# Starting the result's rows as routing weights times the down projection's biases in a fused mixer and expert layer

## The reference

```python
logits = xt @ w_router + b_router                 # 1024 tokens, 32 experts
top_val, top_idx = lax.top_k(logits, 4)
top_w = softmax(top_val)
# each (token, expert) pair, in blocks of one expert:
gate = min(xblk @ w_gate[e] + b_gate[e], 7)
up = clip(xblk @ w_up[e] + b_up[e], -7, 7)
h = (up + 1) * gate * sigmoid(1.702 * gate)
yb = h @ w_down[e] + b_down[e]
y = segment_sum(yb * row_w, row_tok)              # sum over a token's four experts
x = x + gt2 * rms_norm(y, g_post_ffn)
```

## Time and profile before

| | us |
|---|---|
| median of three runs | 2683.56 (2679.57 to 2684.94) |
| the profiled execution | 2680.95 |
| its span, first to last instruction | 2679.1 |
| PE busy | 2422.3 (90%) |
| DVE, ACT, POOL busy | 921.2, 486.7, 413.7 |
| mean granted clock of TensorE | 0.963 of full |

### The profile page before, as it was taken

One profiled execution on the slowest core, in us unless ns is written; L12 is line 12 of the kernel. 1 busy time (PEld: TensorE's weight loads), 2 busy tenths in 40 slices (PEclk: granted clock), 3 DMA queues, 4 the chain that ended last, 5 costly groups with the idle time before them and its releaser, 6 DMA issues.

```text
span 2679.1 us, 35693 instructions
## 1 busy us (share of the span) xinstructions
PE 2422.3 (90%) x11737; PEld 1214.5 (45%) x11784; DVE 921.2 (34%) x1880; ACT 486.7 (18%) x1097; POOL 413.7 (15%) x376
## 2 busy tenths in 40 slices
PE   5999999977884899999999999999999999999992
PEld 3575766663452444444443334433444444434430
DVE  3144536571465222313322233222333323222224
ACT  4121222222441110101110111111111111010111
POOL 5000000004000112111112122122221212212122
PEclk9999999999986899999999999999999999999996
DMA  9112120205022768595899979979877898989875
GB/s 329 32 40 79 40 79 16 87 29 209 32 114 82 253 226 272 157 307 180 269 362 315 321 241 342 356 262 352 260 257 266 292 355 275 332 310 303 310 256 176
DMA packets 213755, 587.60 MB, mean 219 GB/s; under 512 B 20010, under 2 KB 79778, under 8 KB 213698
## 3 DMA queue, kind: packets, MB, share of 16 engines
q1 hardware_dynamic: 131698, 338.21, 34.7%
q10 hardware_dynamic: 53200, 193.02, 20.3%
q0 software_dynamic: 28800, 55.59, 9.8%
HBM read 548.47 MB, written 38.27 MB: 219 GB/s over the span
## 4 chain that ended last, share of the span: by engine, by line
PE 84%; DVE 9%; issue 3%; ACT 1%; POOL 1%; DMA 1%; DVEq 0%; ACTq 0%; SPq 0%; POOLq 0%
PE ps L1582 24%; PE ps L1608 14%; PE ps L1640 12%; PE ps L1658 7%; PE ps L1362 4%; PE ps L1466 4%; PE ps L1358 3%; PE ps L1365 2%; PE ps L1422 2%; PE ps L1551 2%; PE ps L1368 1%; PE ps L1618 1%; PE ps L1334 1%; PE ps L1540 1%; PE ps L1600 1%
## 5 line engine op out<-in xcount | busy, mean ns | idle before, releaser
L1582 PE MATMUL ps<-w_gate_e,xT 128*128 128x512 f32 x736 | 345.8, 592 | 0.0
L1582 PE MATMUL ps<-w_up_e,xT 128*128 128x512 f32 x736 | 345.8, 592 | 0.0
L1640 PE MATMUL ps<-w_down_e,hT 128*128 128x512 f32 x736 | 319.6, 592 | 0.0
L1216 DVE TENSOR_SCALAR oh_gu<-part_e,tab_e 128x128 bf16<-128x128 f32 x48 | 13.9, 290 | 852.1 <-PE ps L1582 543.3
L571 POOL DMA_INDIRECT xg<-xn_rows,gidx x49 | 51.0, 1041 | 1553.5 <-DVE sidx_tab L1207 1490.5
L797 ACT ACTIVATE sig_sb<-gate_sb 128x1024 f32<-128x1024 f32 x47 | 49.7, 1057 | 1160.0 <-DVE gate_sb L1222 1140.5
L1608 PE MATMUL ps<-w_gate_e,xT 128*32 128x256 f32 (+1 forms) x1504 | 236.1, 486 | 0.0
L1608 PE MATMUL ps<-w_up_e,xT 128*32 128x256 f32 (+1 forms) x1504 | 229.9, 474 | 0.0
L1582 PEld LDWEIGHTS ps<-w_up_e,xT 128*128 128x128 f32 x736 | 139.8, 190 | 176.0 <-issue 176.0
L1640 PEld LDWEIGHTS ps<-w_down_e,hT 128*128 128x128 f32 x736 | 139.8, 190 | 168.3 <-issue 165.0
L1582 PEld LDWEIGHTS ps<-w_gate_e,xT 128*128 128x128 f32 x736 | 139.8, 190 | 168.3 <-issue 165.0
(11 more groups left out here) (308 smaller groups left out, 2591.5 us busy)
## 6 DMA issues: line engine op xcount, KB each, us to landing
w_down_e<-in_w_down_dram ACTq DMA_DIRECT2D x368, 512.0 KB, 4.6
w_gate_e<-in_w_gate_dram SPq DMA_DIRECT2D x256, 512.0 KB, 5.6
w_up_e<-in_w_up_dram SPq DMA_DIRECT2D x256, 512.0 KB, 6.8
w_ring<-in_w_ada_dram SPq DMA_DIRECT2D x17, 1024.0 KB, 5.4
w_ring<-in_w_in_dram SPq DMA_DIRECT2D x20, 512.0 KB, 5.1
w_first<-in_w_ada_dram SPq DMA_DIRECT2D x7, 1024.0 KB, 12.5
y_rows<-box POOLq DMA_DIRECT2D x10, 512.0 KB
x_all<-in_x_dram SPq DMA_DIRECT2D x2, 2048.0 KB, 10.7
```

The lines of the kernel that those rows point to most:

```text
L1582: last = T.matmul(ps[:, b, :], xT[:, k, :], wgt[b // 2][:, k, (b % 2) * 512:(b % 2) * 512 + 512], start=False, stop=k == KT - 1)
L1640: last = T.matmul(ps[:, 4 + b, :], hT[:, k, :], wgt[2][:, k, b * 512:b * 512 + 512], start=False, stop=k == KT - 1)
```

## The change

`b_down` leaves the pieces, and the two kinds of bias products leave `down`. The routing weights as float32, `w_full` (tokens x 32), are turned on PE, copied by ACT into `wT` (32 x tokens), and `first_rows(t)` multiplies them by `b_dn` (32 x 512, two halves) into banks 2 and 4. ACT copies each half tile into one of six buffers `y0_sb` and writes it to `y_dram` from its own queue (16 writes of 256 KB). POOL's zeros are left for the two spare blocks alone. Later users of the buffers' memory wait for the writes (`rows_begun`).

```diff
-        bias_rows = region(165, 177)("bias_rows", 3, D)
-        bias_pc = region(181, 187)("bias_pc", 3, D, dt=BF16)
+        bias_rows = region(165, 173)("bias_rows", 2, D)
+        bias_pc = region(181, 185)("bias_pc", 2, D, dt=BF16)
...
-        Y_ZERO = SEQ // P + 2
+        Y_ZERO = 2
+        def rows_begun(eng, bs):
+            for b in bs:
+                eng.wait_ge(y0_out[b], 16 * len(range(b, 2 * TL, len(y0_sb))))
...
-                for m, b in enumerate((b_gate, b_up, b_down)):
+                for m, b in enumerate((b_gate, b_up)):
...
             sp.wait_ge(yx_psum, TL)
+            for h in range(2):
+                sp.dma_start(b_dn[h][:], b_down[0][:, h * HALF:(h + 1) * HALF]).then_inc(b_dn_in, 16)
...
-                pool.dma_start(y_dram[b * P:(b + 1) * P, :], box[0][:, 0:D]).then_inc(y_added, 16)
+                pool.dma_start(y_dram[SEQ + b * P:SEQ + (b + 1) * P, :], box[0][:, 0:D]).then_inc(y_added, 16)
...
             for m in range(3):
                 gather(m)
+            rows_begun(pool, range(len(y0_sb)))
...
@@ ACT @@
+            def weights_turned(t0, nt):
+                act.wait_ge(wT_psum, t0 + nt)
+                A.copy(wT[:, t0:t0 + nt, :], ps[0:NE, 5 + t0 // 4, t0 % 4 * P:(t0 % 4 + nt) * P].rearrange(
+                    "p (t s) -> p t s", s=P)).then_inc(wT_ready, nt)
+            def first_rows(t):
+                for h in range(2):
+                    n = 2 * t + h
+                    b = n % len(y0_sb)
+                    act.wait_ge(y0_psum, n + 1)
+                    if n >= len(y0_sb):
+                        act.wait_ge(y0_out[b], 16 * (n // len(y0_sb)))
+                    A.copy(y0_sb[b][:], ps[:, 2 + 2 * h, :]).then_inc(y0_ready, 1)
+                    act.wait_ge(y0_ready, n + 1)
+                    act.dma_start(y_dram[t * P:(t + 1) * P, h * HALF:(h + 1) * HALF], y0_sb[b][:]
+                                  ).then_inc(y0_out[b], 16)
+            for k in range(2):
+                act.wait_ge(xn2_out[k], 16 * TL // 2)
+            weights_turned(0, 4)
+            for t in range(4):
+                first_rows(t)
+            weights_turned(4, 3)
+            for t in range(4, TL - 1):
+                first_rows(t)
+            weights_turned(TL - 1, 1)
...
             rows_transposed(0)
+            first_rows(TL - 1)
             sigmoid(0)
+            rows_begun(act, range(4, 6))
...
@@ DVE, hidden_transposed and the first item @@
-                one_hot(oh_d, m)
...
             one_hot(oh_gu, 0).then_inc(oh_ready, 1)
+            rows_begun(dve, range(4))
             swiglu(0, link)
...
@@ PE @@
+            def first_rows(t):
+                pe.wait_ge(wT_ready, t + 1)
+                pe.wait_ge(b_dn_in, 32)
+                pe.wait_ge(yx_used, TL)
+                for h in range(2):
+                    if t:
+                        pe.wait_ge(y0_ready, 2 * t + h - 1)
+                    T.matmul(ps[:, 2 + 2 * h, :], wT[:, t, :], b_dn[h][:], start=True, stop=True
+                             ).then_inc(y0_psum, 1)
...
+            weights_turned(0, 4)
+            for t in range(2):
+                first_rows(t)
             pe.wait_ge(diag_tab, 1)
             T.matmul(ps[:, 1, 0:3 * NTAB], ones[:], tab_diag[:].rearrange("p a n -> p (a n)"), start=True, stop=True
...
             def whole_down(m):
-                for b in range(2):
-                    T.matmul(ps[:, 4 + b, :], oh_d[:], bias_pc[:, 2, b * 512:b * 512 + 512], start=True, stop=False)
...
             def small_down(m, parts):
-                for _, N, bank in parts:
-                    C = N * D // P
-                    for j in range(P // N):
-                        T.matmul(ps[N * j:N * j + N, 4 + bank, 0:C], oh_d[:, 0:N], bias_pc[:, 2, j * C:(j + 1) * C],
-                                 start=True, stop=False)
...
+            weights_turned(4, TL - 5)
+            for t in range(2, 5):
+                first_rows(t)
             slot_sums(0)
+            weights_turned(TL - 1, 1)
+            for t in range(5, TL - 1):
+                first_rows(t)
             slot_sums(1)
+            pe.wait_ge(wT_ready, TL)
             rows(0)
+            first_rows(TL - 1)
+            pe.wait_ge(y0_ready, 2 * TL)
             gate_up(0)
```

More of the change, by code:

```diff
@@ L116, in hybrid_block_kernel @@
         gain[0] = r("gain_mix", D)
-        bias_rows = region(165, 177)("bias_rows", 3, D)
-        bias_pc = region(181, 187)("bias_pc", 3, D, dt=BF16)
+        bias_rows = region(165, 173)("bias_rows", 2, D)
+        bias_pc = region(181, 185)("bias_pc", 2, D, dt=BF16)
         rtab_bf = region(187, 189)("rtab_bf", TL, RW, dt=BF16)
         wide_t = region(177, 181)("wide_t", D)
-        r = region(64, 72)
+        b_dn = [region(69, 71)("b_dn0", HALF, parts=NE), region(185, 187)("b_dn1", HALF, parts=NE)]
+        wT = region(161, 165)("wT", TL, P, parts=NE)
+        r = region(149, 157)
+        y0_sb = [r(f"y0_{b}", HALF) for b in range(4)]
+        r = region(177, 181)
+        y0_sb += [r(f"y0_{b}", HALF) for b in range(4, 6)]
+        r = region(64, 69)
         tab_e, tab_b = r("tab_e", NTAB), r("tab_b", NTAB)
@@ L131, in hybrid_block_kernel @@
         logit, mask = r("logit", TL, NE), r("mask", TL, NE)
-        oh_j, wtmp = r("oh_j", TL, NE), r("wtmp", TL, NE)
+        oh_j, w_full = r("oh_j", TL, NE), r("w_full", TL, NE)
         mask_bf, cum_bf = r("mask_bf", TL, NE, dt=BF16), r("cum_bf", TL, NE, dt=BF16)
@@ L140, in hybrid_block_kernel @@
         slot_ids = r("slot_ids", 4, 2 * BLOCK, dt=BF16)
-        oh_gu, oh_d = r("oh_gu", P, dt=BF16), r("oh_d", P, dt=BF16)
+        oh_gu = r("oh_gu", P, dt=BF16)
         w_tab, sidx_tab = r("w_tab", NTAB, 2), r("sidx_tab", NTAB, 3, dt=U32)
@@ L339, in hybrid_block_kernel @@
         hT_psum, hT_ready, d_used, yr_ready = sem("hT_psum"), sem("hT_ready"), sem("d_used"), sem("yr_ready")
+        w_full_ready, wT_psum, wT_ready, y0_psum, y0_ready = (
+            sem(n) for n in ("w_full_ready", "wT_psum", "wT_ready", "y0_psum", "y0_ready"))
+        b_dn_in, y0_out = sem("b_dn_in"), [sem(f"y0_out{b}") for b in range(len(y0_sb))]
         sidx_copied, y_added = sem("sidx_copied"), sem("y_added")
@@ L549, in _ @@
             R3 = slice(0, 3 * NE)
-            pool.wait_ge(brow_in, 16 * 9)
+            pool.wait_ge(brow_in, 16 * 6)
             link(G.memset(bias_pc[:], 0.0))
@@ L1079, in weigh @@
                                          ALU.is_equal, ALU.mult))
-                    link(V.tensor_tensor(rtab[:, t, :], rtab[:, t, :], oh_j[:, t, :], ALU.add))
+                    last = V.tensor_tensor(w_full[:, t, :], w_full[:, t, :], oh_j[:, t, :], ALU.add)
+                    if j < TOP_K - 1:
+                        link(last)
+                last.then_inc(w_full_ready, 1)
+                dve.wait_ge(w_full_ready, t + 1)
+                rest = w_full
                 for piece in range(3):
                     part = rtab_bf[:, t, 3 + piece * NE:3 + (piece + 1) * NE]
-                    link(V.tensor_copy(part, rtab[:, t, :]))
+                    link(V.tensor_copy(part, rest[:, t, :]))
                     if piece < 2:
-                        link(V.tensor_tensor(rtab[:, t, :], rtab[:, t, :], part, ALU.subtract))
+                        link(V.tensor_tensor(rtab[:, t, :], rest[:, t, :], part, ALU.subtract))
+                        rest = rtab
             dve.wait_ge(pieces, 1)
@@ L1496, in places, with weights_turned @@
                 last.then_inc(pos_psum, 1)
+            def weights_turned(t0, nt):
+                pe.wait_ge(xt2_ready, TL)
+                for t in range(t0, t0 + nt):
+                    pe.wait_ge(w_full_ready, t + 1)
+                    last = T.transpose(ps[0:NE, 5 + t // 4, t % 4 * P:(t % 4 + 1) * P], w_full[:, t, :], ident[:])
+                last.then_inc(wT_psum, nt)
+            def first_rows(t):
[5 more added lines that the diff above has]
+                        pe.wait_ge(y0_ready, 2 * t + h - 1)
+                    T.matmul(ps[:, 2 + 2 * h, :], wT[:, t, :], b_dn[h][:], start=True, stop=True).then_inc(y0_psum, 1)
             K_EARLY, K_LATE = [*range(KT - 1, HEADS - 1, -1), *range(HEADS - 1)], [HEADS - 1]
@@ L1640, in whole_down @@
                         last = T.matmul(ps[:, 4 + b, :], hT[:, k, :], wgt[2][:, k, b * 512:b * 512 + 512],
-                                        start=False, stop=k == KT - 1)
+                                        start=k == 0, stop=k == KT - 1)
                     last.then_inc(d_used, 1)
             def small_down(m, parts):
-                for _, N, bank in parts:
-                    C = N * D // P
-                    for j in range(P // N):
-                        T.matmul(ps[N * j:N * j + N, 4 + bank, 0:C], oh_d[:, 0:N], bias_pc[:, 2, j * C:(j + 1) * C],
-                                 start=True, stop=False)
                 for k in range(KT):
@@ L1659, in small_down @@
```

(2 more changed lines are left out.)

2 lines of the change are left out of this document (1 added, 1 removed).

## The result

| | before | after |
|---|---|---|
| median, us (same chip, four executions each) | 2683.77 (2679.57 to 2684.94) | 2659.13 (2657.62 to 2663.03) |
| the profiled execution, its span | 2680.95, 2679.1 | 2663.03, 2660.9 |
| mean granted clock of TensorE | 0.963 | 0.963 |

The kernel became faster: ratio 0.9913, interval 0.9897 to 0.9929, thus 19 to 28 us off 2683.8. The forecast was 2656.6, in a range of 2649 to 2666. The profiled execution of after is the slowest of its four, 3.9 us over their median. Its span is only 18.2 us shorter, so it shows each part, but not the whole gain.

The account below looks back on a forecast made before the run. POOL's bias pieces bound the output projection's start, PE the items, DVE the stretch between router and first item. Terms 8.2 + 18.8 + 0 + 0 = 27.0 us took the median from 2683.56 to 2656.6, range 2649 to 2666.

Parts of the forecast that it names:

- POOL's pieces: POOL's seven bias instructions ahead of the output projection's loop lose a third of their columns: 8.2 us gained, 7.8 to 8.6.
- The memset's ratio: POOL's memset, 2.66 us for 3072 columns, takes 1.80 for 2048; this 32% less was assumed for the other pieces' instructions.
- nothing else would hold DVE: At the output projection's loop, DVE waits for POOL alone, so it moves up with POOL's pieces, and PE with it.
- The items: Bias products leave `down` in 47 items where PE is the limit: 18.8 us gained, 9 to 20.5.
- the one-hot: DVE's one-hot for `down` in the last item, ahead of the hidden rows' copy PE waits for: 0.3 us gained.
- Rival 2: In the items, weight loads become the limit and half of 18.8 stays: 2666 us, chance 0.07.
- The zeros: Eight writes of 512 KB at the start go: 0 us gained, bounds 0 and 1.
- Rival 4: Row writes land late and delay `swiglu(0)`, deciding from 23 us to landing; at 25.2, 2690.5 us, chance 0.03.
- The added stretch: New turns and 16 products fill PE's idle time between router and first item: 0 us, 4 gained to 4 lost.
- a sign of being wrong: In the changed profile, `gate_up(0)` standing behind ACT by more than 3 us would count against the prediction.
- hoped-for faster clock: PE working through the added stretch may get the full clock: 2.4 us in first `gate_up`, some 1.5 ahead of it.
- Rival 1: New products do not fit PE's idle time: half clock, late ACT, 4 for new code, 8 us; 2664.6, chance 0.10.

Follow-up runs that it names:

- e1: Changed kernel with each of POOL's seven bias-piece instructions preceded by one on 1024 columns; 2667.69 us, ratio 0.9937 to the kernel before.
- e9: The changed kernel, unaltered, run again on another chip; 2661.19 us, ratio 0.992 to the kernel before.
- e2: Changed kernel with bias products of the old sizes back in `down`, results overwritten, no one-hot for them; 2673.89 us, ratio 0.9974 to the kernel before.
- e11: Changed kernel with POOL writing all ten blocks of zeros at the start again; 2663.21 us, ratio 0.9926 to the kernel before.
- e3: Changed kernel without the `b_down` part: no turns, products, pieces or row writes, zeros as before; 2663.74 us, ratio 0.9929 to the kernel before.
- e10: Changed kernel with ACT's copies of turned weights moved ahead: tiles 4 to 6 before tile 2's pieces, tile 7 before tile 5; 2657.09 us, ratio 0.991.
- e4: Changed kernel with the 16 new products 128 rows deep instead of 32, same columns, weights scaled by a quarter; 2653.78 us, ratio 0.9888 to the kernel before.
- e5: Changed kernel with both operands of the 16 new products in bf16, still 32 rows deep; 2661.18 us, ratio 0.9927 to the kernel before.
- e8: Changed kernel with bias pieces on DVE and the new products 128 rows deep, together; 2636.19 us, ratio 0.9838 to the kernel before.
- e12: Changed kernel with pieces on DVE, products 128 rows deep and ACT's copies of turned weights ahead; 2640.89 us, ratio 0.9849 to the kernel before.
- e7: Changed kernel with the bias pieces split on DVE, behind the last head, instead of POOL; 2647.45 us, ratio 0.9873 to the kernel before.
- e6: Changed kernel with POOL splitting the bias pieces ahead of `slot_ids`; 2644.95 us, ratio 0.9872 to the kernel before.

## Why the prediction held, and where not

**POOL's pieces: 8.2 forecast, 8.15 measured.** The memset's ratio carried over: 1.80, 1.89 and 4.06 us for 2048 columns. The Trainium skill's 4497 ns for a two-input float32 operation of that size (GPSIMD Engine Reference, Elementwise — side-by-side cycle accounting) is above the 4.06 measured here; the row decides. That nothing else would hold DVE is right too, and e1 moves the path back with the chain.

**The items: 18.8 forecast.** The two profiles of the changed kernel give 16.55 (after) and 17.1 us (e9). The profiles of before and e2, with products in `down`, have 1740.2 and 1737.7 us; the twelve without have 1714.5 to 1726.0, 1719.7 in the mean. That is 19.2 us between the means, and the twelve lie up to 6 us from theirs. The size forecast is within this; it isn't confirmed to better than 3 us. The step of a whole item went from 1.36 us (`rows` to the weights' first product, 1397.06 to 1398.42) to 0.93. In the last item, from the turn of the hidden rows to the weights' first product, it takes 5.82 us where it took 6.79: that is 0.91 for the six products, from start to start, and 0.06 for the one-hot, for which the prediction had 0.3. Rival 2, weights that come late, didn't happen: no wait of PE in the items goes to a transfer in after.

**The zeros: 0, and e11 shows no more.** Rival 4 is excluded by the 2.1 us to landing, where 23 were needed.

**The added stretch: 0 forecast, between 4 gained and 4 lost; it costs 5.8, outside these bounds.** This is the term that was mis-sized. Seven profiles with the new products in the form of the change have 35.3 to 35.6 us there, before and e3 29.5. Its parts, before against after:
- from the tables' product to the first slot sums, 12.64 to 16.67: 4.03 lost, forecast 0 to 1.5. The missed step is ACT's copy of the turned weights, behind the pieces of tiles 2 and 3: PE waits 1.60 for it. The prediction priced ACT by piece and listed `rows(0)`'s wait for the copy of tile 7, but not this one. The other 2.4 are the 1.5 that it had for the lower clock, 0.4 because the turns begin 3.45 us behind the tables' product and not 3.1, and 0.5 because turns and products take 11.6 and not 11.1. A product has the price forecast, 1.71 for 1.72, and no faster clock comes.
- to `rows(0)`, 9.19 to 10.26: 1.07 lost, forecast 0 to 1.2.
- to `gate_up(0)`, 7.68 to 8.42: 0.74, forecast 0 to 1.3. It now stands behind ACT's last piece, copied at 838.33, instead of the one-hot (837.63), by 0.7 and not by the 3 us that would have been a sign of being wrong.

The 0 came from setting a hoped-for faster clock against the late parts. All late parts at half clock, as the prediction had them, are 4.0; the wait for ACT's copy makes 5.6 of them. Rival 1's mechanism is what happened in this stretch, without its 4 us for new code, a term that no row of any run gives. That the clock would rise once PE works through was the argument for 0, and the rows contradict it: PE busy for 32.55 of 40 us in after and for 19.66 of 20 in e10, and the clock at 0.50 in all these windows. The Trainium skill's rule that was quoted beside it, sustained products lift the clock (TensorE: Matmul & The Clock Gate, What you observe), doesn't hold for these rows.

The 5.8 are read from profiles. The times of the whole don't confirm them: the three kernels in which the work is gone or cheaper (e3, e4, e5) have a mean ratio of 0.9915, the changed kernel 0.9913 and 0.9920. Only e4, and e8 and e12 beside e7, are faster by about that much.

**The sum.** 8.15 + 19.2 - 5.8 = 21.5 us with the measured sizes, 27.0 forecast. The ratio gives 23.3 (19 to 28) for after and 21.5 (16 to 27) for e9. So the sum was 5.5 us too high, and the stretch, priced too low, makes 5.8 of it. That the forecast of 2656.6 lies only 2.5 us under the median of after is in part luck of its four executions; from e9's, 2661.19, it is 4.6 off. Two details of the forecast don't come out. The bounds of its terms, added up, give 2649.5 to 2670.8 and not 2651 to 2662. And from the first `gate_up` to the last `down` it had 18 us less, where after has 14.5 and e9 17.5; the difference in after is the 2.08 above and the items.

## What to carry to other kernels

Filling an engine's idle time with work needs two prices: the time at the clock that the stretch has now, and the order in which the helper engine hands things back; both have to fit, and a copy that opens the next group of products belongs ahead of the last group's copies out of PSUM (e10: 2.3 us of the stretch). When work leaves a chain on the path, look at where the chain starts: moving POOL's pieces up (e6) gave some 11 us more where making them shorter gave 8. And put the operation where it costs least on the path: 32 experts' biases into the result once, instead of one product with each of 47 items, is worth 17 to 19 us in the items for some 6 in one stretch.

## What the runs showed of the chip

The same 16 products of 512 columns left TensorE at the lower clock when they were 32 rows deep (after: 0.50 and 0.50, PE busy for 32.6 of 40 us), and ran at 0.68 and 0.91 when they were 128 deep (e4, PE busy for 26.4). e10 had 0.50 even with PE busy for 19.66 of 20 us. e4 also has four times as many turns, so this shows that the pair of edits raises the clock, not which of the two.

Executions of one kernel scatter by 5 to 17 us. A possible part of it can be seen between kernels whose items are the same: after PE has been idle, the first products run at the lower clock in some profiles and not in others. One such place is the same item in after and in e8. PE's timeline, first of after:

```profile
1365.33 1.87 PE L1676 MATMUL ps<-bias_pc,oh_gu 128*64 128x512 bf16 x12 [2.09 <-issue]
1367.13 1.80 PE L1684 MATMUL ps<-w_gate_e,xT 128*64 128x512 f32 x4
```

and of e8:

```profile
1339.72 1.19 PE L1679 MATMUL ps<-bias_pc,oh_gu 128*64 128x512 bf16 x12 [2.08 <-issue]
1340.85 1.08 PE L1687 MATMUL ps<-w_gate_e,xT 128*64 128x512 f32 x4
```

From one turn of hidden rows to the next, that item takes 43.65 us in after, 43.72 in e9 and 42.24 in e8. Another one (PE idle for 2.16 us ahead of it) took 46.07 in before, 44.34 in e10 and 42.70 in after and e9, where the change accounts for 0.43. A few such places, 1.4 to 3 us each, are as large as the effects looked for in e3 and e5. The two profiles of the changed kernel agree at both, so that this also sets one execution of a kernel apart from another isn't shown. The start of POOL's pieces differs too, from 641 to 651 us in kernels whose work up to there is the same.
